# A two-block transformer kernel: normed input for the MLP's later groups, and wide products in their up units

## The reference

```
sh_a, sc_a, g_a, sh_m, sc_m, g_m = split(silu(c) @ w_ada + b_ada)       # 6 x 2048
x  = x + g_a * (concat(attn, pool) @ w_out)
hm = rms_norm(x, norm_mlp_w) * (1 + sc_m) + sh_m
x  = x + g_m * (square(relu(hm @ w_up)) @ w_down)                         # 2048 -> 8192 -> 2048
return rms_norm(x, final_norm_w)
```

## Time and profile before

| what | value |
|---|---|
| median of three runs | 1679.48 us (1677.22 to 1681.92) |
| profiled execution, its own time | 1680.85 us |
| its span | 1678.4 us |
| PE busy | 1610.2 us (96%) |
| PE weight loads busy | 1499.6 us (89%) |
| VectorE busy | 1191.4 us (71%) |
| ScalarE busy | 766.8 us (46%) |
| mean HBM read | 221 GB/s |
| mean granted TensorE clock | 0.988 |

### The profile page before, as it was taken

One profiled execution on the slowest core, in us unless ns is written; L12 is line 12 of the kernel. 1 busy time (PEld: TensorE's weight loads), 2 busy tenths in 40 slices (PEclk: granted clock), 3 DMA queues, 4 the chain that ended last, 5 costly groups with the idle time before them and its releaser, 6 DMA issues.

```text
span 1678.4 us, 33242 instructions
## 1 busy us (share of the span) xinstructions
PE 1610.2 (96%) x12218; PEld 1499.6 (89%) x12218; DVE 1191.4 (71%) x1754; ACT 766.8 (46%) x1044; POOL 35.0 (2%) x50
## 2 busy tenths in 40 slices
PE   4799999999999999999899999999999999999997
PEld 4689999899999998888799999899988998899986
DVE  5477777588888775677766666776677766556786
ACT  4254444344445554445455454345533554345542
POOL 0000000000001000000000100000000000000000
PEclk9899999899999999999999999999999999999998
DMA  5788887688986768732355665986589655655553
GB/s 188 257 285 278 290 287 259 240 321 321 340 321 206 234 196 309 289 118 86 103 159 180 195 204 179 269 272 196 185 256 276 197 184 188 189 163 186 178 186 112
DMA packets 94552, 372.65 MB, mean 222 GB/s; under 512 B 10016, under 2 KB 10544, under 8 KB 83968
## 3 DMA queue, kind: packets, MB, share of 16 engines
q1 hardware_dynamic: 88656, 333.87, 60.6%
q10 hardware_dynamic: 4608, 33.56, 5.5%
q0 software_dynamic: 1200, 4.02, 0.7%
HBM read 369.30 MB, written 2.10 MB: 221 GB/s over the span
## 4 chain that ended last, share of the span: by engine, by line
issue 72%; PE 19%; DVE 7%; ACT 1%; DMA 0%; POOL 0%; SPq 0%; POOLq 0%; DVEq 0%; ACTq 0%
PE G L432 5%; PE G L433 5%; PE G L434 5%; DVE lo L1209 2%; PE M L719 1%; PE S L595 1%; DVE blk L1209 1%; PE ADA L474 1%; DVE sm L1579 1%; DVE blk L1592 1%; PE S L693 1%; DVE t L1264 0%; PE S L694 0%; DMA ident<-ident_dram 0%; DVE actA L1238 0%
## 5 line engine op out<-in xcount | busy, mean ns | idle before, releaser
L1209 DVE TENSOR_TENSOR lo<-raw,hi 128x1024 fp32r<-128x1024 f32 x496 | 607.4, 1225 | 233.1 <-ACT hi L862 219.9
L862 ACT ACTIVATE hi<-raw 128x1024 fp32r<-128x1024 f32 x496 | 526.2, 1061 | 501.4 <-PE G L434 283.8
L432 PE MATMUL G<-actA,hi 128*128 128x256 f32 (+1 forms) x2368 | 682.9, 288 | 4.7 <-DVE actA L1209 4.0
L433 PE MATMUL G<-actA,lo 128*128 128x256 f32 (+1 forms) x2368 | 671.0, 283 | 0.0
L434 PE MATMUL G<-actA,hi 128*128 128x256 f32 x2368 | 670.8, 283 | 0.0
L432 PEld LDWEIGHTS G<-actA,hi 128*128 128x128 f32 x2368 | 451.2, 191 | 38.1 <-issue 29.9
L433 PEld LDWEIGHTS G<-actA,lo 128*128 128x128 f32 x2368 | 451.2, 191 | 0.3
L434 PEld LDWEIGHTS G<-actA,hi 128*128 128x128 f32 x2368 | 450.4, 190 | 0.0
L458 PE MATMUL G<-actB,hi 128*128 128x512 f32 x1024 | 355.5, 391 | 0.4 <-DVE lo L1209 0.3
L459 PE MATMUL G<-actB,lo 128*128 128x256 f32 x1024 | 286.6, 280 | 0.0
L458 PEld LDWEIGHTS G<-actB,hi 128*128 128x128 f32 x1024 | 191.5, 187 | 42.9 <-issue 1.1
(11 more groups left out here) (210 smaller groups left out, 1210.8 us busy)
## 6 DMA issues: line engine op xcount, KB each, us to landing
raw<-stream_dram SPq DMA_DIRECT2D x496, 512.0 KB, 4.3
ada_raw<-w_ada_dram SPq DMA_DIRECT2D x64, 1024.0 KB, 7.5
ada_raw<-w_ada_dram ACTq DMA_DIRECT2D x32, 1024.0 KB, 6.4
resid<-xT_dram SPq DMA_DIRECT2D x4, 512.0 KB, 5.6
ctx_tok<-ctx_tok_dram SPq DMA_DIRECT2D x1, 2048.0 KB, 13.2
W<-ctxT_dram POOLq DMA_DIRECT2D x16, 128.0 KB, 3.7
out_dram<-resid SPq DMA_DIRECT2D x4, 512.0 KB, 2.7
ada_raw<-pool_w_dram POOLq DMA_DIRECT2D x1, 1024.0 KB, 7.6
```

The source lines that it names most:

```text
L432: pe.matmul(wide, hi[:, slot, cols], x[:, k, 0:T + extra], start=(k == 0), stop=False, skip_group_check=True)
L433: pe.matmul(wide, lo[:, slot, cols], x[:, k, 0:T + extra], start=False, stop=False, skip_group_check=True)
L862: return act.activation(dst, src, ACT.Copy)
L1209: return dve.tensor_tensor(dst, a, b, op)
```

## The change

Group 0's up units stay. In group 0's down units VectorE and ScalarE now also write the normed, scaled and shifted input, split in hi and lo, to `actA` (in the memory that `actU` no longer needs), one tile per unit. The up units of groups 1 to 3 use `pair_unit` on `actA`. Their evacuation is another: ScalarE copies the bank's second half, VectorE adds the first and makes max(v, 0) * v, ScalarE writes the rounded value to `actB` and VectorE the low part. The gate loads and the gate's VectorE instructions move from the down units of groups 0 and 1 to those of groups 1 and 2; `gate_sums` stays before group 3. Group 0's down units are written out without a loop on ScalarE and VectorE.

```diff
 # SyncE
             for g in range(2):
-                weights(at, U_MLP + 2 * KT * g + KT)
+                weights(at, U_MLP + 2 * KT * (g + 1) + KT)
                 for i in range(8):
-                    at = U_MLP + 2 * KT * g + KT + 2 * i
+                    at = U_MLP + 2 * KT * (g + 1) + KT + 2 * i
                     for n in range(4):
                         weight(n, 2 * at + 8 + n)
                         if n == 1 and 1 < 8 * g + i + 1 < KT:
                             gate_load(8 * g + i + 1)
 # TensorE
+                elif g == 1:
+                    pair_unit(At(base), 0, actA, inA, 3 * KT)
+                    pair_unit(At(base), 1, actA)
+                    pair_units(7, base + 2, actA)
                 else:
-                    up_units(8, base)
+                    pair_units(8, base, actA)
 # ScalarE, groups 1 to 3 (group 0 as before)
+                            split(at, j, 0)
+                            split(at, j)
+                            act.wait_ge(evac_done, at.unit(j))
+                            copy(scaled[:, j], G[j % 2][:, T:2 * T]).then_inc(second_copied, 1)
+                            act.wait_ge(second_copied, turn.next("second"))
+                            high(actB[:, bass.ds(i * 2 + j, 1), 0:T], t4[:, 2 + j:3 + j])
 # ScalarE, down units of group 0
+                if not g:
+                    for k in range(KT):
+                        split(At(base + KT), k, 0)
+                        split(At(base + KT), k)
+                        shifted_high(actA[:, k, 0:T], t4[:, k % 2], adav[:, 0, SH_M + k:SH_M + k + 1])
+                    continue
 # VectorE, groups 1 to 3 (group 0 as before)
+                            split(at, j, 0)
+                            dve.wait_ge(second_copied, turn.next("second"))
+                            tt(scaled[:, j], scaled[:, j], G[j % 2][:, 0:T], ALU.add).then_inc(evac_done, 1)
+                            turn.next("evac_done")
+                            evacuated(at, j)
+                            dve.scalar_tensor_tensor(t4[:, 2 + j], scaled[:, j], 0.0, scaled[:, j], ALU.max, ALU.mult).then_inc(nt_ready, 1)
+                            own(nt_ready)
+                            split(at, j)
+                            low(actB[:, u, 0:T], actB[:, u, T:2 * T], t4[:, 2 + j:3 + j], inB)
 # VectorE, down units of group 0
+                    for k in range(KT):
+                        split(at, k, 0)
+                        down(at, k, slice(k, k + 1), False, None)
+                        dve.scalar_tensor_tensor(t4[:, k % 2], resid[:, k], scale_m[:, k:k + 1], rstd_bc, ALU.mult,
+                                                 ALU.mult).then_inc(nt_ready, 1)
+                        own(nt_ready)
+                        split(at, k)
+                        shifted_low(actA[:, k, 0:T], actA[:, k, T:2 * T], t4[:, k % 2], adav[:, 0, SH_M + k:SH_M + k + 1], inA)
 # VectorE, down units with gate sums: `if g < 2` becomes `elif g < 3`, (4 * g + 1) becomes (4 * (g - 1) + 1)
...
```

More of the change, by code:

```diff
@@ L59 @@
     "act up": {"relu_done": 2, "nt_hi": 2, "hi_done": 4},
+    "act up pair": {"second": 2, "nt": 2, "nt_hi": 2, "hi_done": 4},
     "act down": {"hi_done": 4},
@@ L65 @@
     "dve up": {"relu_done": 2, "seq": 2, "lo_done": 4, "nt": 2, "inB": 2},
+    "dve up pair": {"second": 2, "evac_done": 2, "nt_ready": 2, "lo_done": 4, "nt": 2, "inB": 2},
     "dve down": {"seq": 2, "lo_done": 4},
@@ L247, in program @@
         gate_full = [sem(f"gate_full{i}") for i in range(2)]
+        second_copied = sem("second_copied")
         out_ready, out_sent = sem("out_ready"), sem("out_sent")
@@ L1167, in _ @@
                 base = U_MLP + 2 * KT * g
[L1168 to L1178, removed]
@@ L1179, in _ @@
-                last = g == MLP_GROUPS - 1
+                if g:
+                    with turn.lap(act, 8, "act up pair") as i:
+                        for j in range(2):
+                            at = At(base, 2, i)
+                            split(at, j, 0)
[4 more added lines that the diff above has]
+                            high(actB[:, bass.ds(i * 2 + j, 1), 0:T], t4[:, 2 + j:3 + j])
+                else:
+                    with turn.lap(act, 8, "act up") as i:
+                        for j in range(2):
+                            at = At(base, 2, i)
+                            split(at, j, 0)
+                            split(at, j)
+                            act.wait_ge(inB, i * 2 + (KT * (1 + g) + 8 + j - 1))
+                            evacuated(at, j)
+                            act.activation(t4[:, j], scaled[:, j], ACT.Relu, bias=sm[:, 40 + j:41 + j]).then_inc(relu_done, 1)
+                            own(relu_done)
+                            act.activation(actB[:, bass.ds(i * 2 + j, 1), 0:T], t4[:, j:j + 1], ACT.Square).then_inc(nt_hi, 1)
+                            own(nt_hi)
@@ L1705, in _ @@
                 base = U_MLP + 2 * KT * g
[L1706 to L1716, removed]
+                if g:
+                    with turn.lap(dve, 8, "dve up pair") as i:
+                        for j in range(2):
+                            at, u = At(base, 2, i), bass.ds(i * 2 + j, 1)
+                            split(at, j, 0)
+                            dve.wait_ge(second_copied, turn.next("second"))
+                            tt(scaled[:, j], scaled[:, j], G[j % 2][:, 0:T], ALU.add).then_inc(evac_done, 1)
+                            turn.next("evac_done")
+                            evacuated(at, j)
+                            dve.scalar_tensor_tensor(t4[:, 2 + j], scaled[:, j], 0.0, scaled[:, j], ALU.max, ALU.mult).then_inc(nt_ready, 1)
+                            own(nt_ready)
+                            split(at, j)
+                            low(actB[:, u, 0:T], actB[:, u, T:2 * T], t4[:, 2 + j:3 + j], inB)
+                else:
+                    with turn.lap(dve, 8, "dve up") as i:
+                        for j in range(2):
+                            at, u = At(base, 2, i), bass.ds(i * 2 + j, 1)
+                            split(at, j, 0)
+                            summed(at, j)
+                            dve.reduce_sum(sm[:, 40 + j:41 + j], G[j % 2][:, T:T + 2], AX.X)
+                            tt(scaled[:, j], G[j % 2][:, 0:T], rstd_bc, ALU.mult).then_inc(evac_done, 1)
+                            split(at, j)
+                            dve.wait_ge(relu_done, turn.next("relu_done"))
+                            seq(tt(t4[:, 2 + j], t4[:, j], t4[:, j], ALU.mult))
+                            low(actB[:, u, 0:T], actB[:, u, T:2 * T], t4[:, 2 + j:3 + j], inB)
@@ L1738, in _ @@
                     dve.wait_ge(acc_zero, 1)
-                if g < 2:
-                    if g == 0:
+                if g == 0:
+                    at = At(base + KT)
+                    for k in range(KT):
[6 more added lines that the diff above has]
+                        shifted_low(actA[:, k, 0:T], actA[:, k, T:2 * T], t4[:, k % 2], adav[:, 0, SH_M + k:SH_M + k + 1], inA)
+                elif g < 3:
+                    if g == 1:
                         dve.wait_ge(gate_zero, 1)
@@ L1746, in _ @@
                                 slot = j // 2
-                                dve.wait_ge(gate_full[slot], i * 16 + 16 * (4 * g + 1))
+                                dve.wait_ge(gate_full[slot], i * 16 + 16 * (4 * (g - 1) + 1))
                                 dve.scalar_tensor_tensor(gate_part, ada_raw[:, slot].rearrange("p k n -> p (k n)"),
-                                                         gate_c[:, bass.ds(i * 76 + (8 * 38 * g + 38 * slot + 6), 1)], gate_part,
+                                                         gate_c[:, bass.ds(i * 76 + (8 * 38 * (g - 1) + 38 * slot + 6), 1)], gate_part,
                                                          ALU.mult, ALU.add).then_inc(gate_taken, 1)
                                 own(gate_taken)
[L1752 to L1755, removed]
                 else:
```

## The result

| | before | changed |
|---|---|---|
| median | 1681.88 us (11 runs, 1677.22 to 1686.50) | 1690.88 us (11 runs, 1683.48 to 1692.99) |
| profiled execution | 1680.85 us, span 1678.4 | 1686.56 us, span 1684.8 |
| ratio to before | | 1.0050, 95% interval 1.0037 to 1.0063 |

The changed kernel is slower by some 8.4 us (0.37 to 0.63%). I had forecast 1681 and a range up to 1687; the time lies outside. The profiled executions are 5.7 us apart.

What follows compares the result with a forecast made beforehand. PE was taken to bound the kernel, other engines counting only when late for it. Terms of -9.92, +6.6, +3.2, +0.3 and +1.3 summed to +1.5 us on 1680.85, less 1.37: 1681.0 us, range 1675 to 1687.

Steps and rivals of the forecast that it cites:

- Part 1: Up products of groups 1 to 3: in the down units' form each stage takes 88.75 us, -9.92 us in all.
- a rival of this kind: Up stages: wide products bring nothing with actA, only 4 extra columns go; 1.4 us gained, about 1689.5; chance 0.02.
- the 0.96 us of the second gate stage: Second gate stage's excess over the first, taken as PE stall that stays; bounds -1 and +1.
- Part 2: New up units: ScalarE and VectorE can feed them, 3.8 us plus some 0.5 of waits under 5.55; cost 0.
- Part 3: Norming and splitting in group 0's down units: hidden by PE; cost 0, bounds 0 and 0.5 us.
- Part 4: Gate loads and sums one group later: PE waits before group 3's up units, +6.6 us, bounds 5.0 and 8.4.
- Part 5: Around the gate stall: 32 single-column matmuls run at low clock, +3.2 us; later clock loss +0.3.
- The clock loss behind it: Dense products after the gate sums: 1.5 to 3 us lost where 1.49 was before; +0.3 us, bounds 0 and 1.5.
- Part 6: Entry of group 2's up stage: weight halves come late for the pair form, +1.3 us, bounds 0 and 1.3.
- the ledger's +1.5: Sum of all terms over the whole kernel: -9.92 + 6.6 + 3.2 + 0.3 + 1.3 us.
- entry, stall, wait and clock: Terms for group 2's up entry +1.3, second gate stage's 0.96 staying, gate wait +6.6, clock loss +0.3 us.
- The range: Whole kernel: 1675 to 1687 us, the low end taking in part of a faster rival, the high end a late gate.

Runs made afterwards that it cites:

- e4_aligned: Changed kernel with actA allocated behind lo, so actB, raw, hi, lo and actA start at multiples of 16 KB; one run, 1687.77 us.
- e6_weights_off: Changed kernel with actB, then actA, allocated ahead of raw, hi and lo, leaving hi and lo 128 bytes past a 16 KB multiple; one run, 1685.98 us.
- e9_view_late: e1_sums_late with the normed input in a view of actA that starts 128 bytes later; 1674.59 us, 0.9959 of the kernel before.
- e1_sums_late: Changed kernel with PE's gate_sums moved behind group 3's up units, ahead of its down units; 1678.8 us, 0.9981 of the kernel before.
- e3_narrow_entry: Changed kernel with the first down unit of groups 1 to 3 as three 256-column products per tile; one run, 1690.71 us.
- e8_pause_entry: Changed kernel with 4 (group 1) and 16 (group 2) single-column products put between up and down units; one run, 1696.83 us.
- e5: Changed kernel with the edits of e1_sums_late and e4_aligned together; 1679.71 us, 0.9989 of the kernel before.
- e11: Changed kernel with only the normed input's view moved by 128 bytes, gate_sums left ahead of group 3's up units; 1686.24 us, 1.0026 of the kernel before.
- e12: e9_view_late with the view 64 bytes later instead of 128; one run, 1675.74 us.
- e10: e9_view_late with the ninth gate load issued amid group 2's up units instead of at group 1's down end; 1675.28 us, 0.9964 of the kernel before.

## Why the prediction was wrong, by its own steps

- **Part 1, the step that failed.** I wrote that "the new form is the form of the down units, so an up stage should take 88.75 us" and booked -9.92. The sentence takes the spacing of a matmul from its shape. The runs show that the same shape takes 5.547, 5.617 or 5.653 us a unit here, by the distance of its operands and by what PE did before: the up units took 5.617 (gain 2.2 per stage, 6.6 in all), and the down units of groups 1 to 3, which I had not even listed as touched, went from 5.547 to 5.653: +5.1. Together -1.5 instead of -9.92, 8.4 us off. e4_aligned, e6_weights_off and e9_view_late show the distance as the cause. I had a rival of this kind, that the wide product brings nothing on `actA`, at a chance of 0.02. Its 1689.5 us is near the 1690.88 measured by luck: it left the up stages at almost 92 us, and they took 89.87. (The Trainium skill's formula that leaned its way, TensorE: Matmul & The Clock Gate, "Back-to-back issue gap", goes by columns alone, and columns did not change between the spacings.) The earlier trace rows had the wide form only at `actB`'s distance, behind narrow products; I read three equal stages as three confirmations and they were one case. I also read the 0.96 us of the second gate stage as idle PE. Its row has 89.28 us busy in 89.71, so only 0.43 is idle; the rest is PE busy at the slower spacing, as in this unit, which needs 5.547 us elsewhere:

```profile
1275.20:1280.85 5.65, 5.65 (x33) 1.00 0.92 253
```

  So the profile before already held the same shape at two spacings.
- **Part 2 right.** PE never waited for the new evacuation; the chain fits in the unit. **Part 3 right**: group 0's down stage is 88.75.
- **Part 4 right in kind and size.** 5.9 against 6.6 forecast; 5.75 to 7.4 over the seven profiles of kernels with the wait, VectorE's gate instruction last in each that was read.
- **Part 5 right.** The sums took 6.98 us at the low clock; +3.2 as forecast. The rule of the Trainium skill for weight loads (TensorE: Matmul & The Clock Gate, "LDWEIGHTS (loading the stationary operand)", columns / 1.2) agrees with the trace at full clock only: 32 in 3.63 us there (e1_sums_late), in 6.98 at the low one. The clock loss behind it was 1.4, not more than before.
- **Part 6 not in the changed kernel's profile, but there.** Group 2's up stage took 91.15 us in e1_sums_late and 91.18 in e3_narrow_entry, 1.3 more than group 1's, and 90.40 in e8_pause_entry, against 89.88 in the changed kernel. The spacing up to there is the same in all four, so it does not hide this stall: it comes in some executions and not in others. The 0.96 us of the second gate stage are another matter: with slow down units no profile has a wait there.
- So the ledger's +1.5 became +6.6 in the stages (6.4 in the spans, 5.7 in the executions' own times): 8.4 too little for the products; 1.3, 1.0, 0.7 and 0.4 too much for entry, stall, wait and clock.
- **The range.** Its upper end was made of mishaps on the path I knew. None of the terms allowed a stage without an edit to get slower while PE is busy.

Still open: the mechanism inside PE behind the spacings, what flips a stage between 5.547 and 5.653, and why the slow one was left behind the single-column matmuls in five profiles (e1, e5, e8, e11, e12) and not in a sixth (e10).

## What to carry to other kernels

Where PE streams without a gap, the time per tile is measured at one placement of the operands and behind one predecessor; moving the same form to another buffer is a new measurement, and the stages that follow it count too. Read the spacing from stage lengths, not from the durations of instructions, and look at the stages that nobody edited. A sum that is needed late should be waited for late: moving `gate_sums` by one stage was worth 11.6 us, more than the 9.92 I had booked for the products.

## What the runs showed of the hardware that I had not expected

- A unit of 16 x (512 + 256) columns took 88.75 / 16 = 5.547 us, 5.617 with the moving operand 128 bytes off the distance to the weights at which this was measured, 5.653 with 64 bytes off, in patterns of a few tiles that repeat through a stage.
- At the good distance there were two lasting states, 5.547 and 5.653 us per unit; which one a stage takes depends on what ran before it and on short stalls.
- Single-column matmuls and their weight loads follow the granted clock: 32 in 3.63 us with loads of 192 ns at 1.00, in 6.98 us with loads of 333 ns at 0.50.
- Allocating `actA` behind `lo`, which moves the four buffers in between by 32,896 bytes, made the kernel before 0.21% slower, by its profile ahead of the MLP; the place was not found.
